# Attention steps of a pair in another order, and the last value keys turned in the middle of a projection

## The chip, the cores and the metric

The kernel runs on one core of a Trainium2 chip. The metric is the device time in microseconds (us) of one execution; the times shown are medians over several executions.

## The reference, cut to what matters

The whole computation is a hybrid block (a state-space mixer and an attention side by side, a gated feed-forward) and a second layer. The change touches the attention of the first block only: 16 heads of 64 features, 16 leading meta tokens and 1024 tokens.

```python
def block(args):
    i, qi = args
    q_pos = i * Q_BLOCK + jnp.arange(Q_BLOCK)
    valid = (key_pos[None, :] < q_pos[:, None]) & (key_pos[None, :] >= pad)
    zlog = jnp.einsum('bqhd,bkhd->bhqk', qi, kp) * scale
    log_beta = jax.nn.log_sigmoid(zlog)
    log_keep = jnp.where(valid, log_beta - zlog, 0.0)
    after = lax.cumsum(log_keep, axis=3, reverse=True) - log_keep
    w = jnp.where(valid, jnp.exp(log_beta + after), 0.0)
    return jnp.einsum('bhqk,bkhd->bqhd', w, vp)

o = lax.map(block, (jnp.arange(nb), qb))        # nb = 9 blocks of 128 queries
```

A query of block j sees the 16 meta keys and up to 128 x j others, so the nine blocks of a head are of very different length. The results of the blocks don't depend on each other. What is left of the stick after each key is a running product over the keys, and the output is a sum over keys of what is left times the step from one value to the next.

## The kernel before

TensorE is PE here, VectorE DVE, ScalarE ACT, GpSimd POOL, and SyncE (SP) issues the DMAs. Numbers are split into a high and a low half of 16 bits, so that a product of two is three matmuls (`PASSES`).

`attention_phase` works through 72 steps (`STEPS`): 8 pairs of heads (`PAIRS`), and for each the nine query blocks (`NSTEP`), j = 0 to 8 in rising order. `Step(n)` holds the numbers of a step: `p` the pair, `j` the block, `rows` (16 for j=0, else 128), `keys` = 16 + 128 j, of which at most 1024 fit in one pair of PSUM banks (`wide`); for j=8 the 16 that are left over are computed at j=3 (`z_more`) and kept in `left_more`. `slot` = j % 3 names the buffer. Each engine has a loop of its own over the steps `s`, all in program order:

- PE: `scores(s)` (queries by keys, both heads), at j=1 `turn_v` (turns the last value keys, from `steps`), then one group `linear(s + 9)` of a projection of 24 matmuls of 348 columns (`GROUPS` = 9 of them make the queries, keys and values of the next pair; in pair 7 they are those of the first w_out blocks), `turn_w(s - 1)` (turns the 32 meta columns of the step before), `values(s - 2)` (6 j matmuls on the turned left-overs, and one on the meta keys, L1274).
- ACT: `odds(s)` (sigmoid of the scores, one for each head), at j=1 `copy_v`, `left_high(s, 0)`, each third step `weight_high`, `place(s + 9)` (evicts the projection), `left_high(s, 1)` or at j=0 `values_high`, `copy_w(s - 1)`, `split_high(s - 1)`, `store(s - 2)`, at j=4 `square`.
- DVE: at j=2 `split_values`, then `split_weights(s - 2)`, `scan(s, 0)`, `scan(s, 1)` (the running product, 16 + 128 j columns), `left_low(s, 0)` or at j=0 `v_steps`, `low(s + 9)` for the queries and keys, `left_low(s, 1)` or at j=0 `values_low`, at the steps of `NORMED_AT` `norm_chunk`, each third step `weight_low`, from pair 2 at j=5 `add_square`.
- SP: `turn_left` for both heads (a transposing DMA of what is left, from one of three slots of `sent`), at j=0 `turn_values`, each third step the load of a weight block.
- POOL: the low halves of the normed chunks of the mixer's output (`low`, one for each `NORMED_AT`), and at the end the splits of two w_out blocks, each part behind a wait for a projection: `pool.wait_ge(s_lin, NT * (QKV_B + EARLY - SLOTS + s + 1))` is met when group 77 and group 80 are done, which PE does in steps 68 and 71.

What orders the engines among each other around the change:

```python
pe.wait_ge(s_keep, 2 * n)              # scores(n): odds of step n-1 are out
pe.wait_ge(s_copied, t.turn())         # turn_w(n): copy_w(n-1) has emptied turn_ps
pe.wait_ge(s_scan, 2 * n + 2)          # turn_w(n): both scans of step n
pe.wait_ge(s_copied, v_turn(p))        # turn_v(p): copy_w of the last step of pair p-1
pe.wait_ge(s_o, n)                     # values(n): store(n-1) has emptied o_ps
pe.wait_ge(*landed(t.sent(a)))         # values(n): the turned left-overs are there
pe.wait_ge(s_wlo, n + 1)               # values(n), last matmul: split_weights(n)
act.wait_ge(*landed(e - SENT_SLOTS))   # left_high: the slot of three sends ago
```

`split_weights(n)` stands on DVE at the start of step n + 2, behind all the work of step n + 1. The sends are numbered in a pair by `sent`: 17 (`SENDS`), the values first.

## Time and profile before

| | |
|---|---|
| median of 3 runs | 2336.02 us |
| lowest run | 2334.57 us |
| profiled execution | 2333.68 us, span 2331.9 us |
| PE busy | 2202.1 us, 94% |
| DVE busy | 1592.7 us, 68% |
| ACT busy | 1036.3 us, 44% |
| POOL busy | 607.0 us, 26% |
| mean granted clock of PE | 0.982 |
| attention steps, first scores to the next stage | 367.81 to 828.75 us of the span |

The page gives the busy time of an engine as a share of the span. A view of windows gives the busy time in stretches, with the clock granted to PE (1.00 is 2.4 GHz). A timeline row is a start, a length, engine, line, operation, output<-input with the shape, how many alike, and in brackets the idle time before it with what ended it. Matmuls overlap in the pipeline, so the distance from start to start tells more than a length.

### The profile page before, as it was taken

What the parts mean: (1) busy time and instruction counts of PE and PEld (TensorE: products, weight loads), DVE (VectorE), ACT (ScalarE), POOL (GpSimd) and SP (SyncE); (2) the same over time, 40 slices, a digit from 0 to 9 for tenths busy, and PEclk for the clock granted to TensorE, in tenths of its full rate; (3) what the DMA queues carried; (4) which work ended last, traced back from release to release, by engine and by line L of the source; (5) the groups of instructions that cost most, each with busy time, mean ns of one, the idle gap of its engine ahead of it and who ended that gap; (6) DMA issues with size and microseconds to landing.
All of it is one profiled execution on the core that took longest, in us unless ns stands there. A gap on an engine that the chain in (4) does not pass through costs nothing. (4 is left out here: it accounts for less than half of the span.)

```text
span 2331.9 us, 44629 instructions
## 1 busy us (share of the span) xinstructions
PE 2202.1 (94%) x18332; PEld 1411.5 (61%) x18332; DVE 1592.7 (68%) x2016; ACT 1036.3 (44%) x1883; POOL 607.0 (26%) x379
## 2 busy tenths in 40 slices
PE   7999998899999889989999999999999999999997
PEld 4666665555555556656666665458644445588846
DVE  7876887888888855787777774257688484236544
ACT  3226765667666643434444443235543232124221
POOL 3555762000000120064333331000256442001060
PEclk9999999999999989999999999999999999989998
DMA  3113213676766631211111113326333612032412
GB/s 130 48 52 101 82 55 71 116 130 125 135 126 126 110 107 63 94 41 50 55 55 59 55 51 118 101 74 212 124 102 104 212 55 82 23 101 72 158 60 73
DMA packets 279377, 216.24 MB, mean 93 GB/s; under 512 B 194752, under 2 KB 245120, under 8 KB 277776
## 3 DMA queue, kind: packets, MB, share of 16 engines
q1 hardware_dynamic: 279184, 213.51, 34.0%
q8 instruction: 140, 2.29, 0.4%
q14 instruction: 53, 0.43, 0.1%
HBM read 145.77 MB, written 25.76 MB: 74 GB/s over the span
## 5 line engine op out<-in xcount | busy, mean ns | idle before, releaser
L1519 DVE TENSOR_TENSOR_SCAN att_left<-att_left,att_unseen_prefix 16x16 f32<-16x16 f32 (+5 forms) x144 | 177.9, 1276 | 28.2 <-ACT att_left L1332 26.9
L2912 PE MATMUL ps<-second_x_hi,whi_z 128*128 128x512 f16 (+1 forms) x480 | 179.1, 373 | 2.6 <-DVE second_x_lo L1740 1.4
L1219 PE MATMUL ps<-x_hi,whi_z 128*128 128x348 f16 x560 | 176.7, 315 | 4.7 <-DVE att_q L1450 4.7
L2913 PE MATMUL ps<-second_x_lo,whi_z 128*128 128x512 f16 (+1 forms) x480 | 178.8, 372 | 0.0
L2914 PE MATMUL ps<-second_x_hi,wlo_z 128*128 128x512 f16 (+1 forms) x480 | 178.8, 372 | 0.0
L1221 PE MATMUL ps<-x_hi,wlo_z 128*128 128x348 f16 x560 | 175.3, 313 | 0.0
L1220 PE MATMUL ps<-x_lo,whi_z 128*128 128x348 f16 x560 | 175.3, 313 | 0.0
L1352 ACT ACTIVATE att_left_split<-att_left 128x256 f16<-128x256 f32 (+7 forms) x128 | 87.2, 681 | 111.9 <-DVE att_left L1519 111.1
L2215 PE MATMUL ps<-x_lo,whi_z 128*128 128x342 f16 x432 | 133.2, 308 | 0.0
L2214 PE MATMUL ps<-x_hi,whi_z 128*128 128x342 f16 x432 | 132.8, 308 | 0.0
L2216 PE MATMUL ps<-x_hi,wlo_z 128*128 128x342 f16 x432 | 132.6, 307 | 0.0
L1478 DVE SCALAR_TENSOR_TENSOR att_left_split<-att_left,att_left_split 128x256 f16<-128x256 f32 (+7 forms) x128 | 105.9, 828 | 12.7 <-ACT att_left_split L1352 12.0
L2881 POOL TENSOR_TENSOR wlo_z<-wraw_z,whi_z 128x1024 f16<-128x1024 f32 x28 | 66.3, 2367 | 178.7 <-ACT whi_z L3097 178.7
L3097 ACT ACTIVATE whi_z<-wraw_z 128x1024 f16<-128x1024 f32 x28 | 29.6, 1056 | 132.6 <-PE ps L2914 116.3
L216 PE MATMUL ps<-x_hi,whi_xbc 128*128 128x348 f16 x264 | 83.1, 315 | 4.7 <-DVE x_lo L484 4.7
L1197 POOL TENSOR_SCALAR wraw_z<-wraw_z 128x1024 f32<-128x1024 f32 x2 | 2.9, 1460 | 317.0 <-DMA wraw_z<-in_w_out 317.0
L2912 PEld LDWEIGHTS ps<-second_x_hi,whi_z 128*128 128x128 f16 x480 | 47.0, 98 | 62.4 <-issue 6.5
L217 PE MATMUL ps<-x_lo,whi_xbc 128*128 128x348 f16 x264 | 82.9, 314 | 0.0
L218 PE MATMUL ps<-x_hi,wlo_xbc 128*128 128x348 f16 x264 | 82.9, 314 | 0.0
L2913 PEld LDWEIGHTS ps<-second_x_lo,whi_z 128*128 128x128 f16 x480 | 47.1, 98 | 53.6 <-issue 3.9
L1219 PEld LDWEIGHTS ps<-x_hi,whi_z 128*128 128x128 f16 x560 | 54.8, 98 | 40.9 <-issue 13.9
L2380 DVE SCALAR_TENSOR_TENSOR wlo_z<-wraw_z,whi_z 128x512 f16<-128x512 f32 x72 | 58.2, 831 | 31.0 <-ACT whi_z L2292 31.0
(657 smaller groups left out, 6438.7 us busy)
## 6 DMA issues: line engine op xcount, KB each, us to landing
wraw_z<-in_w_second SPq DMA_DIRECT2D x30, 512.0 KB, 3.6
wraw_z<-in_w_up SPq DMA_DIRECT2D x26, 512.0 KB, 3.5
wraw_z<-in_w_qkv SPq DMA_DIRECT2D x24, 512.0 KB, 4.2
wraw_z<-in_w_down SPq DMA_DIRECT2D x20, 512.0 KB, 4.3
raw_down<-in_w_down SPq DMA_DIRECT2D x20, 512.0 KB, 4.1
seg<-dt_a_sums SPq DMA_DIRECT2D x18, 512.0 KB, 5.1
wraw_z<-in_w_up SPq DMA_DIRECT2D x36, 256.0 KB, 3.7
second_work<-parked_units SPq DMA_DIRECT2D x7, 1280.0 KB, 6.0
```

The costliest lines, as they stand in the source:

```text
L1219: nc.tensor.matmul(lin_ps(g), hi, xhi, start=(kb == 0), stop=False)
L1220: nc.tensor.matmul(lin_ps(g), hi, xlo, start=False, stop=False)
L1221: last = nc.tensor.matmul(lin_ps(g), lo, xhi, start=False, stop=(kb == DB - 1))
L1352: nc.scalar.activation(sent[:, e % SENT_SLOTS, 0:P * t.j], of_head(t, a, 0, P * t.j), ACT.Copy, scale=PSCALE).then_inc(s_left_hi, 1)
L1478: nc.vector.scalar_tensor_tensor(low_, of_head(t, a, 0, P * t.j), PSCALE, high, ALU.mult, ALU.subtract).then_inc(s_left_lo, 1)
L1519: nc.vector.tensor_tensor_scan(x, x, unseen, 1.0, ALU.mult, ALU.max).then_inc(s_scan, 1)
L2214: nc.tensor.matmul(out, hi, xhi, start=begin, stop=False, skip_group_check=True)
L2215: nc.tensor.matmul(out, hi, xlo, start=False, stop=False, skip_group_check=True)
L2216: of_block = nc.tensor.matmul(out, lo, xhi, start=False, stop=stop, skip_group_check=True)
L2912: nc.tensor.matmul(out, hi, xhi, start=(j == 0), stop=False)
L2913: nc.tensor.matmul(out, hi, xlo, start=False, stop=False)
L2914: return nc.tensor.matmul(out, lo, xhi, start=False, stop=(j == DB - 1))
```

## The change

The steps of a pair no longer run in rising order of block length. `Step` takes its block from a table by its place `i` in the pair: `ORDER` for pairs 0 to 6 and `LAST_ORDER` for pair 7. What was bound to j=0 to 5 of a pair (the value steps and their send, `turn_v`, `copy_v`, `split_values`, `square`) is bound to the same place i; `add_square` goes from place 5 to 6. The 16 left-over scores of j=8 (`z_more`) are computed at i=0 instead of at j=3 and lie at the end of the second bank. `NORMED_AT` names other steps. `turn_v` stands between the fourth and the fifth of the eight parts of the step's projection instead of ahead of it. The number, shapes and operands of all instructions stay. Of the diff, the hunks that only put `t.i` or `V_SENT[p]` in place of `t.j` or `SENDS * p` are left out.

```diff
+ORDER, LAST_ORDER = (0, 7, 2, 6, 1, 8, 3, 4, 5), (0, 7, 5, 6, 4, 8, 3, 1, 2)
+SENDS = 2 * NSTEP - 1
+
+
+def sent_order(blocks):
+
+    counts = [2 * (j > 0) + (i == 0) for i, j in enumerate(blocks)]
+    return [sum(counts[:i]) for i in range(NSTEP)]
+
+
+SENT_OF = sent_order(ORDER), sent_order(LAST_ORDER)
+V_SENT = [SENDS * p for p in range(PAIRS)]
...
-        self.n, self.p, self.j = n, n // NSTEP, n % NSTEP
+        self.n, self.p, self.i = n, n // NSTEP, n % NSTEP
+        self.j = (ORDER if self.p < PAIRS - 1 else LAST_ORDER)[self.i]
+        self.stash = self.i == 0
...
-        return SENDS * self.p + 2 * self.j - 1 + a
+        return SENDS * self.p + SENT_OF[self.p == PAIRS - 1][self.i] + a
...
-NORMED_AT = {1: 3, 2: 4, 3: 5, 10: 6, 11: 7}
+NORMED_AT = {2: 3, 4: 4, 6: 5, 11: 6, 13: 7}
...
-        z_more = flat[:, 2 * BANK:6 * BANK].rearrange("p (a n) -> p a n", a=2)[:, :, BANK:BANK + META]
+        z_more = flat[:, 2 * BANK:6 * BANK].rearrange("p (a n) -> p a n", a=2)[:, :, 2 * BANK - META:2 * BANK]
...
-                    if t.j == 3:
+                    if t.stash:
...
-                    if t.j == 1:
-                        pe.wait_ge(*landed(SENDS * t.p))
+                    if t.i == 0:
+                        pe.wait_ge(s_vlo, t.p + 1)
+                    if t.i <= 1 and t.j:
+                        pe.wait_ge(*landed(V_SENT[t.p]))
...
-                    else:
-                        pe.wait_ge(s_vlo, t.p + 1)
...
-                    if s < STEPS and ATT[s].j == 1:
+                    if s + GROUPS < (QKV_B + EARLY) * NT:
+                        linear(s + GROUPS, 0, DB // 2)
+                    if s < STEPS and ATT[s].i == 1:
                         turn_v(ATT[s].p)
                     if s + GROUPS < (QKV_B + EARLY) * NT:
-                        linear(s + GROUPS, 0, DB)
+                        linear(s + GROUPS, DB // 2, DB)
...
-                    if ATT[s].j == LAG:
+                    if ATT[s].i == LAG:
                         split_values(ATT[s].p)
...
-                    if ATT[s].j == 0:
+                    if ATT[s].j:
+                        left_low(s, 0)
+                    if ATT[s].i == 0:
                         v_steps(ATT[s].p)
-                    else:
-                        left_low(s, 0)
...
-                    if p >= 1 and ATT[s].j == 5:
+                    if p >= 1 and ATT[s].i == 6:
                         add_square(p)
```

On DVE, from the value steps of pair 3 on, to the split of the meta weights of the pair's first step (the 32x16 row; `att_left` 128x144 is block 1, 128x912 block 7). Before:

```order
L1484 TENSOR_TENSOR att_left_split<-att_v_steps,att_left_split 128x1024
L1455 SCALAR_TENSOR_TENSOR wlo_z<-wraw_z,whi_z 128x1024
L1462 TENSOR_TENSOR att_w_meta_split<-att_w_meta,att_w_meta_split 32x128
L1519 SCALAR_TENSOR_TENSOR att_left<-att_left,att_unseen_prefix 128x144 x2
L1478 SCALAR_TENSOR_TENSOR att_left_split<-att_left,att_left_split 128x128
L1450 SCALAR_TENSOR_TENSOR att_q<-ps,att_q 128x348
L1478 SCALAR_TENSOR_TENSOR att_left_split<-att_left,att_left_split 128x128
L1469 CAST att_v_meta_split<-att_v_meta 32x128
L1470 CAST att_v_meta_split<-att_v_meta 32x128
L1472 TENSOR_TENSOR att_v_meta_split<-att_v_meta,att_v_meta_split 32x128
L1462 TENSOR_TENSOR att_w_meta_split<-att_w_meta,att_w_meta_split 32x16
```

The same stretch of the changed kernel:

```order
L1500 TENSOR_TENSOR att_left_split<-att_v_steps,att_left_split 128x1024
L1471 SCALAR_TENSOR_TENSOR wlo_z<-wraw_z,whi_z 128x1024
L1478 TENSOR_TENSOR att_w_meta_split<-att_w_meta,att_w_meta_split 32x128
L1535 SCALAR_TENSOR_TENSOR att_left<-att_left,att_unseen_prefix 128x912 x2
L1494 SCALAR_TENSOR_TENSOR att_left_split<-att_left,att_left_split 128x896
L1466 SCALAR_TENSOR_TENSOR att_q<-ps,att_q 128x348
L1494 SCALAR_TENSOR_TENSOR att_left_split<-att_left,att_left_split 128x896
L1485 CAST att_v_meta_split<-att_v_meta 32x128
L1486 CAST att_v_meta_split<-att_v_meta 32x128
L1488 TENSOR_TENSOR att_v_meta_split<-att_v_meta,att_v_meta_split 32x128
L1478 TENSOR_TENSOR att_w_meta_split<-att_w_meta,att_w_meta_split 32x16
```

The block that stands between the value steps and this split has become the one of 912 columns instead of the one of 144.

On PE, where pair 3's last value keys are turned (`att_v_steps`), between the scores of the second step and its projection. Before:

```order
L1235 MATMUL ps<-att_k_odd,att_q_odd 128x144 x6
L1248 MATMUL ps<-ident,att_v_steps 32x128
L1219 MATMUL ps<-x_hi,whi_z 128x348
L1220 MATMUL ps<-x_lo,whi_z 128x348
L1221 MATMUL ps<-x_hi,wlo_z 128x348
```

In the changed kernel:

```order
L1236 MATMUL ps<-x_hi,wlo_z 128x348
L1263 MATMUL ps<-ident,att_v_steps 32x128
L1234 MATMUL ps<-x_hi,whi_z 128x348
L1235 MATMUL ps<-x_lo,whi_z 128x348
L1236 MATMUL ps<-x_hi,wlo_z 128x348
```

The turn now has twelve of the projection's matmuls ahead of it and twelve behind it.

On PE at the end of the stage, behind the last projection (the values of the last three steps). Before:

```order
L1254 MATMUL ps<-ident,att_left 32x128
L1268 MATMUL ps<-att_left_turned,att_v_tokens 64x128 x36
L1274 MATMUL ps<-att_w_meta_split,att_v_meta_split 128x128
L1254 MATMUL ps<-ident,att_left 32x128
L1268 MATMUL ps<-att_left_turned,att_v_tokens 64x128 x42
L1274 MATMUL ps<-att_w_meta_split,att_v_meta_split 128x128
L1268 MATMUL ps<-att_left_turned,att_v_tokens 64x128 x48
L1274 MATMUL ps<-att_w_meta_split,att_v_meta_split 128x128
```

In the changed kernel:

```order
L1269 MATMUL ps<-ident,att_left 32x128
L1285 MATMUL ps<-att_left_turned,att_v_tokens 64x128 x18
L1289 MATMUL ps<-att_w_meta_split,att_v_meta_split 128x128
L1269 MATMUL ps<-ident,att_left 32x128
L1285 MATMUL ps<-att_left_turned,att_v_tokens 64x128 x6
L1289 MATMUL ps<-att_w_meta_split,att_v_meta_split 128x128
L1285 MATMUL ps<-att_left_turned,att_v_tokens 64x128 x12
L1289 MATMUL ps<-att_w_meta_split,att_v_meta_split 128x128
```

Behind the last projection stand the values of blocks 3, 1 and 2 instead of those of blocks 6, 7 and 8.

## Rows read from the trace of the kernel before

**Rows 1.** The page: busy us, share of the span, instructions

```profile
PE 2202.1 (94%) x18332; PEld 1411.5 (61%) x18332; DVE 1592.7 (68%) x2016; ACT 1036.3 (44%) x1883; POOL 607.0 (26%) x379
```

**Rows 2.** Windows: pairs 0, 1, 3, then 7, tail (width, PE, PEld, DVE, ACT, POOL, clock, DMA)

```profile
367.81:423.73 55.92, 48.88 (x454) 29.64 (x449) 48.46 (x58) 35.13 (x80) 8.74 (x5) 0.94 0.47 96
423.73:482.98 59.25, 51.43 (x547) 32.20 (x542) 50.66 (x63) 38.87 (x90) 4.34 (x2) 0.97 0.68 114
...
537.06:591.14 54.08, 49.78 (x548) 31.73 (x543) 45.76 (x62) 37.05 (x88) 0.00 (x0) 1.00 0.66 127
...
753.54:809.01 55.47, 49.87 (x504) 31.07 (x498) 44.75 (x53) 33.96 (x84) 7.68 (x4) 0.97 0.61 107
809.01:828.75 19.74, 7.72 (x133) 6.21 (x131) 10.81 (x8) 7.36 (x18) 3.17 (x2) 0.65 0.61 101
```

**Rows 3.** Timeline of PE where pair 3 begins (start, length, line, idle before)

```profile
534.88 1.20 PE L1268 MATMUL ps<-att_left_turned,att_v_tokens 128*64 128x128 f16 x36 [0.26 <-ACT z L1389]
...
536.90 0.23 PE L1235 MATMUL ps<-att_k_odd,att_q_odd 64*16 64x16 f16 x6 [0.66 <-ACT att_left L1332]
...
541.72 0.28 PE L1254 MATMUL ps<-ident,att_left 128*32 128x128 f32 x1 [0.95 <-ACT att_w_meta L1345]
542.71 1.36 PE L1268 MATMUL ps<-att_left_turned,att_v_tokens 128*64 128x128 f16 x42 [0.70 <-ACT z L1389]
...
546.26 0.28 PE L1248 MATMUL ps<-ident,att_v_steps 128*32 128x128 f32 x1 [1.73 <-ACT att_w_meta L1345]
```

**Rows 4.** Timeline of PE, step 7 of pair 3, from its projection to the next scores

```profile
578.60 0.32 PE L1219 MATMUL ps<-x_hi,whi_z 128*128 128x348 f16 x1
...
582.15 0.27 PE L1254 MATMUL ps<-ident,att_left 128*32 128x128 f32 x1
582.35 1.03 PE L1268 MATMUL ps<-att_left_turned,att_v_tokens 128*64 128x128 f16 x30
...
583.47 1.47 PE L1235 MATMUL ps<-att_k_odd,att_q_odd 64*128 64x512 f16 x12
```

**Rows 5.** Timeline of DVE: block 7 of pair 2, then the value steps of pair 3

```profile
528.70 4.01 DVE L1519 TENSOR_TENSOR_SCAN att_left<-att_left,att_unseen_prefix 128x912 f32<-128x912 f32 x2
532.62 2.19 DVE L1478 SCALAR_TENSOR_TENSOR att_left_split<-att_left,att_left_split 128x896 f16<-128x896 f32 x2
...
543.31 1.19 DVE L1527 TENSOR_TENSOR att_v_steps<-att_v 128x1024 f32<-128x1024 f32 x1
...
546.08 1.22 DVE L1484 TENSOR_TENSOR att_left_split<-att_v_steps,att_left_split 128x1024 f16<-128x1024 f32 x1 [0.70 <-ACT att_left_split L1359]
547.22 1.22 DVE L1455 SCALAR_TENSOR_TENSOR wlo_z<-wraw_z,whi_z 128x1024 f16<-128x1024 f32 x1
548.47 0.28 DVE L1462 TENSOR_TENSOR att_w_meta_split<-att_w_meta,att_w_meta_split 32x128 f16<-32x128 f32 x1
```

**Rows 6.** Timeline of ACT behind the second scan of block 8

```profile
540.46 1.06 ACT L1352 ACTIVATE att_left_split<-att_left 128x1024 f16<-128x1024 f32 x1 [0.81 <-DVE att_left L1519]
541.42 0.25 ACT L1345 ACTIVATE att_w_meta<-ps 32x128 f32<-32x128 f32 x1
...
542.56 0.22 ACT L1332 ACTIVATE att_left<-ps 16x16 f32<-16x16 f32 x2
```

**Rows 7.** The line that issues turn_left, pair 7: from issue to landing

```profile
DMA to landing us min/median/max: 2.4/4.2/5.7
```

**Rows 8.** Timeline of PE, values of block 2 in pair 0

```profile
396.28 0.29 PE L1274 MATMUL ps<-att_w_meta_split,att_v_meta_split 96*128 96x128 f16 x1 [3.25 <-DVE att_w_meta_split L1462]
```

**Rows 9.** Timeline of PE, values of block 8 in the tail

```profile
824.99 2.77 PE L1268 MATMUL ps<-att_left_turned,att_v_tokens 128*64 128x128 f16 x48 [3.06 <-DMA att_left_turned<-att_left_split]
```

**Rows 10.** Timelines of DVE and POOL, block 5 of pair 7

```profile
790.30 4.26 DVE L1478 SCALAR_TENSOR_TENSOR att_left_split<-att_left,att_left_split 128x640 f16<-128x640 f32 x2
794.49 2.06 DVE L1536 TENSOR_TENSOR mixed_squares<-mixed_squares,rs_ssd_y 128x1026 f32<-128x1026 f32 x1
...
791.30 2.58 POOL L1202 TENSOR_TENSOR wlo_z<-wraw_z,whi_z 128x1024 f16<-128x1024 f32 x1
```

More of the change, by code:

```diff
@@ L1055 @@
 NORMED_EARLY = 3
-NORMED_AT = {1: 3, 2: 4, 3: 5, 10: 6, 11: 7}
+NORMED_AT = {2: 3, 4: 4, 6: 5, 11: 6, 13: 7}
 PSCALE = 32768.0
-SENDS = 2 * NSTEP - 1
 SENT_SLOTS, SENT_SIGNALS = 3, 4
@@ L1149, in turn_values @@
                 def turn_values(p):
-                    e = SENDS * p
+                    e = V_SENT[p]
                     sp.wait_ge(s_left_lo, e + 1)
@@ L1226, in scores @@
                     t = ATT[n]
-                    if t.j == 0:
+                    if t.i == 0:
                         pe.wait_ge(s_low, 2 * NT * (t.p + 1))
@@ L1259, in values @@
                         pe.wait_ge(s_o, n)
-                    if t.j == 1:
-                        pe.wait_ge(*landed(SENDS * t.p))
+                    if t.i == 0:
+                        pe.wait_ge(s_vlo, t.p + 1)
+                    if t.i <= 1 and t.j:
+                        pe.wait_ge(*landed(V_SENT[t.p]))
                     if t.j:
@@ L1325, in odds @@
                                 act.wait_ge(s_left_lo, ATT[n - 3].sent(1) + 1)
-                    if a == 1 and t.j == 3:
+                    if a == 1 and t.stash:
                         nc.scalar.activation(left_more[:, 0:META], z_more[:, 0, :], ACT.Sigmoid, scale=-0.125)
@@ L1354, in values_high @@
                 def values_high(p):
-                    e = SENDS * p
+                    e = V_SENT[p]
                     act.wait_ge(s_steps, p + 1)
@@ L1386, in store @@
                     act.wait_ge(s_pv, n + 1)
-                    if t.j == 0:
+                    if t.i == 0:
                         act.wait_ge(N.cut, t.p + 1)
@@ L1419, in _ @@
                             odds(s, a)
-                        if ATT[s].j == 1:
+                        if ATT[s].i == 1:
                             copy_v(ATT[s].p)
@@ L1429, in _ @@
                         chunk_high(NORMED_AT[s - 1])
-                    if s < STEPS:
-                        if ATT[s].j:
-                            left_high(s, 1)
-                        else:
-                            values_high(ATT[s].p)
+                    if s < STEPS and ATT[s].j:
+                        left_high(s, 1)
+                    if s < STEPS and ATT[s].i == 0:
+                        values_high(ATT[s].p)
                     if 1 <= s <= STEPS:
@@ L1439, in _ @@
                         store(s - LAG)
-                    if s < STEPS and ATT[s].p and ATT[s].j == 4:
+                    if s < STEPS and ATT[s].p and ATT[s].i == 4:
                         square(ATT[s].p - 1)
@@ L1480, in values_low @@
                 def values_low(p):
-                    e = SENDS * p
+                    e = V_SENT[p]
                     high, low_ = (sent[:, e % SENT_SLOTS, i * SEQ:(i + 1) * SEQ] for i in range(2))
@@ L1547, in _ @@
                     scan(s, 1)
-                    if ATT[s].j == 0:
+                    if ATT[s].j:
+                        left_low(s, 0)
+                    if ATT[s].i == 0:
                         v_steps(ATT[s].p)
-                    else:
-                        left_low(s, 0)
                     if s + GROUPS in SPLIT:
@@ L1555, in _ @@
                         left_low(s, 1)
-                    else:
+                    if ATT[s].i == 0:
                         values_low(ATT[s].p)
```

## Prediction

> **What bounds the kernel now.** The page's busy table comes first: TensorE (PE) is busy for 94% of the span [rows 1], so an order of steps can give back only the time in which PE waits. The windows cut by pair say how much that is in the attention stage [rows 2]: pair 0 takes 55.92 us, pair 1 59.25, each of pairs 2 to 6 takes 54.08 with 49.78 us of PE work, pair 7 takes 55.47 up to the end of its last projection, and a tail of 19.74 us with 7.72 us of PE work follows. So PE waits 4.3 us in each steady pair and 12 us in the tail, 54 us in the whole stage (widths less PE's work: 7.0 + 7.8 + 21.5 + 5.6 + 12.0).
>
> PE's timeline shows where [rows 3]: behind the longest block (j=8) at a pair's start it waits 0.26 us for ScalarE's (ACT) store, 0.95 for ACT's copy ahead of turn_w, 0.70 for the next store, and 1.73 for the copy ahead of turn_v; with 0.66 for the scores of j=0 that is 4.3. In blocks 1 to 6 there is no wait: that step is a projection of 3.55 us (578.60 to 582.15), turn_w 0.20, the values of block j, 0.165 us x j + 0.29 (j=5: 582.35 to 583.47), and the scores [rows 4].
>
> DVE's pace is behind these waits. From start to start VectorE (DVE) needs for j=7 3.92 us of scans and 2.2 of low halves, and at j=0 1.56 for v_steps, 1.14 for values_low and 1.25 for the weights' low half; each step has a split_weights of 0.3 [rows 5]. j=8 (7.0) and j=0 (5.9) are neighbours, so PE outruns DVE there. ACT sits in the loop: high half of head 1 (0.96), then copy_w, split_high and store (1.14) before it can turn the next scores into odds [rows 6].
>
> **The change, part by part.** Nothing is added or removed: the same instructions with the same shapes. PE's work stays 49.78 us a steady pair. Only waits move. I follow the three engines with the durations of rows 4 to 6 (scans and halves scaled by block length), each step counted from the end of its scores on PE, until a pair repeats itself.
>
> *Order 0,7,2,6,1,8,3,4,5.* PE step lengths without waits become 5.98 (i=0 to 1), 5.4, 4.9, 5.5, 5.8, 5.6, 5.0, 6.3, 4.9 us. In this order DVE enters i=0 3.7 us late: ACT is 3.5 us late since i=8 (j=5) ends with head 1's high half and the 1.14 us tail. From there:
> - i=0: DVE ends 5.8 us later, at 9.5 us, or 3.5 after the scores of i=1. turn_v is wanted 1.77 us (four of eight products of the projection) into i=1, and its copy_w is done at 0.8: the old 1.73 us wait is gone. It would be so even at the old place but for 0.8 us, as no j=8 stands ahead of it.
> - i=1 (j=7) and the first work of i=2: 3.92 + 2.1 + 0.45 (low) + 0.78 (split_values) + 0.17 = 7.4 us on DVE. Here the new wait arises. The values step of j=0 needs split_values and split_weights of i=0, which DVE reaches at 3.7 + 5.8 + 7.4 = 16.9 us; PE is there at 5.98 + 5.40 + 3.66 = 15.0. A wait of 1.9 us. Queued behind it on PE are the scores of j=6; for these ACT and DVE then wait, which gives DVE its time back (late by 1.7 at i=3).
> - i=3 (j=6, 3.4 + 1.7 + low and weights 2.0): DVE ends about 4.1 after the scores of i=4, PE wants the split at 4.2: no wait, or 0.35 if head 1's high half of i=2 first waits for a slot (three slots; a turn lands after a median 4.2 us [rows 7]).
> - i=4 holds ACT's square (0.94), i=5 is j=8: DVE ends at 4.8 after the scores of i=6, and the short values of j=1 want it at 4.05: 0.77 us. i=6 with weights and add_square leaves DVE at 5.5, wanted at 5.2: 0.28.
> New waits: 1.9 + 0.2 + 0.8 + 0.3 = 3.2 us a pair against 4.3 before, so 1.1 x 5 = **5.5 us** for pairs 2 to 6. A lower bound is no wait at all (21.5 us gained), an upper one is the largest that DVE's split has cost so far, 3.25 us [rows 8], in place of the 1.9 (a loss of 0.25 a pair).
>
> *NORMED_AT.* Each chunk costs DVE 1.2 us, and then POOL's low half makes a DVE instruction wait. In pair 0 they now fall on i=2, 4 and 6; the one at i=2 is followed by j=6, and by my count PE waits 1.2 + 2.3 + 2.5 + 1.2 us, with the clock at its lower level for a while as now (granted clock 0.94 in pair 0, 0.97 in pair 1, 1.00 after [rows 2]). I get 55.4 us against 55.92: **0.5**. Pair 1: waits of 1.9 + 2.8 + 1.8 and 1.0 of clock, 57.3 against 59.25: **2.0**.
>
> *LAST_ORDER 0,7,5,6,4,8,3,1,2.* In the tail of before DVE first ends j=8, its turn lands, and the 48 values products of j=8 take 2.77 us, at 1.2 GHz, the lower level, where 30 at 2.4 GHz took 1.03 (granted clock 0.65 in the tail); the wait for the turn ahead of them is 3.06 us [rows 2, 4, 9]. Now block 2 is last. After the last projection: evict and high half 0.9, DVE's low half behind POOL until about 3.8, a turn of 2.4 to 4.2, 12 products and the split 1.0 to 1.4, store and entry of the next stage 1.0: 8.2 us instead of 19.74, 11.5 less. Against it: values of 12 more block lengths run ahead of the last projection, 12 x 0.165 = 2.0; and POOL's splits of the last two w_out blocks start with fixed projections (i=5 and i=8 of pair 7). At 790 us POOL's work made DVE's two halves take 4.2 us instead of 1.55, and 0.84 more behind them: 3.5 in all [rows 10]. In before it hit j=5 and PE lost 2.2. Now it hits j=8: DVE ends at 15.0 where PE wants it at about 10: 5 us, and i=2, i=3, i=4 wait 1.05, 0.15 and 0.75. With 2 us for a clock that falls in such a wait I get 57.8 us to the end of the last projection (55.47 before) and 8.2 behind it: 66.0 against 75.2, **9.2 us**.
>
> The Trainium skill (SBUF — State Buffer, Who interferes with whom) has the port pair of these two engines as an exclusive lock, held for a whole instruction. The trace agrees: two low halves that take 1.55 us elsewhere take 4.2 beside POOL's 2.58 us subtraction. By the lock each of POOL's three instructions there could hold DVE for its whole length; at 2.58 each that would be 7.7 us instead of 3.5, and the gain would be 4.2 us smaller.
>
> Sum: 5.5 + 0.5 + 2.0 + 9.2 = 17.2 us. The profiled execution took 2333.7 us (span 2331.9); the median of the runs is 2336.0, 2.3 above it. So 2316.5 for a run like the profiled one, 2318.8 from the median; I say **2318**.
>
> **Rivals.**
> - *DVE keeps up (0.1).* ACT's lateness at i=8 is less than I count, DVE enters i=0 2 us earlier, and the waits at i=2, 6 and 7 vanish. For it: DVE's work is 45.8 us of 49.8 [rows 2]. Against it: that is 92%, and i=0 and i=1 together have 13.2 us for 11.4 of PE. Gain 21.5 + 3 + 5 + 12 = 41: 2294.
> - *Only the tail counts (0.22).* The new waits in a pair equal the old 4.3, as each late point costs 0.4 more. Then pairs 0 to 6 give nothing and pair 7 gives 5 to 10: 2328.
> - *The clock falls in each pair: slower (0.08).* Now the steady pairs keep a granted clock of 1.00 with 4.3 us of waits; pair 1 has 0.97, a price of 0.03 x 59.25 = 1.8 us [rows 2]. If the waits at i=2 and at i=6 each bring that, 14 x 1.8 = 25 us are lost against 17 gained: 2335 + 8 = 2343. It decides from 17.2 / 14 = 1.2 us a wait. Against it: 1.73 with 0.95 and 0.70 ahead of it leaves the steady clock at 1.00 [rows 2, 3], and 1.9 stands alone. The Trainium skill (TensorE: Matmul & The Clock Gate, Part 1: The HAM clock gate) says that idleness brings the throttled state, 1.2 GHz, and activity ends it; that pairs 0 and 1 and the tail lose clock and steady pairs don't agrees with it.
> - *My forecast (0.6):* 2306 to 2326.
>
> **How the numbers follow.** The forecast holds 0.6 in 2306 to 2326; with most of the tail-only case and half of the first rival the range is 2300 to 2334. A change of 2% (47 us), about what a measurement of this kernel can tell from no change, needs seven eighths of the stage's 54 us of waits: 0.03 for faster. Slower by as much needs six times the loss of the clock rival: 0.01. The rest, 0.96, is within 2%, most of it on the faster side.
>
> **What would show it.** Right: pairs 2 to 6 take 52.5 to 53.5 us; PE's longest wait in each is ahead of the values split of j=0, for DVE's split_weights, 1 to 3 us; turn_v waits for nothing; in pair 7 PE waits about 5 us in the step of j=3; 7 to 9.5 us pass from the last projection to the next stage. Wrong: if the granted clock of the steady pairs falls below 0.99; if pairs take 54 us or more; or if the wait at i=2 is absent, which would mean that ACT is not 3.5 us late at a pair's start.

## The result, and the profile after

The changed kernel takes 2318.82 us (median; 2317.35 to 2320.57), 0.993 of the kernel before, with a 95% interval of 0.9906 to 0.9954: 0.5 to 0.9% faster. Two of the four executions of the kernel before, 2565.34 and 8615.65 us, lie far off and are left out of that ratio; the other two took 2334.57 and 2336.02. The profiled execution took 2320.57 us (span 2318.8) against 2333.68 (span 2331.9), 13.1 us less. The forecast was 2318 us, yet 0.96 of its chance went to a change of less than 2%, which it took to be about what can't be told from none, and the time did change by three times what the interval allows for noise. In the long series of the experiments the kernel before had a median of 2333.7 us, so the gain is 15 to 17 us.

The windows of after, cut like those of [rows 2]: pairs 0 and 1, 2 to 6, 7, and the tail up to the first product of the next stage (width, PE, PEld, DVE, ACT, POOL, granted clock, DMA share, GB/s).

```profile
367.82:423.54 55.72, 49.53 (x490) 30.27 (x485) 50.03 (x58) 35.46 (x80) 9.39 (x4) 0.97 0.59 108
423.54:480.69 57.15, 51.57 (x548) 32.08 (x542) 51.56 (x64) 38.83 (x91) 5.05 (x2) 0.97 0.61 125
480.69:532.98 52.29, 49.79 (x548) 31.66 (x542) 45.13 (x61) 36.20 (x88) 0.00 (x0) 1.00 0.73 129
532.98:586.36 53.38, 49.85 (x548) 31.62 (x542) 46.13 (x63) 36.64 (x88) 0.00 (x0) 1.00 0.63 130
...
693.95:747.15 53.20, 49.93 (x547) 31.64 (x541) 45.99 (x62) 36.58 (x88) 0.00 (x0) 1.00 0.64 130
747.15:805.58 58.43, 52.34 (x552) 32.94 (x546) 48.60 (x57) 36.77 (x88) 9.14 (x4) 0.94 0.66 119
805.58:811.54 5.96, 2.62 (x43) 1.48 (x40) 2.73 (x3) 3.37 (x12) 3.21 (x2) 0.96 0.23 47
```

The stage lasts 443.72 us (367.82 to 811.54) against 460.94, that is 17.2 us less. Set beside [rows 2]: pair 0 gives 0.2 us, pair 1 2.1, pair 7 and the tail together 10.8 (64.39 against 75.21), and pairs 2 to 6 4.1: they take 266.5 us, 53.3 each, against 270.6. Behind the stage 4.1 us of it are lost again in this execution.

PE's waits in a steady pair (pair 3), the rows of its timeline in that window with an idle time ahead of them:

```profile
549.90 0.17 PE L1289 MATMUL ps<-att_w_meta_split,att_v_meta_split 96*128 96x16 f16 x1 [1.68 <-DVE att_w_meta_split L1478]
561.42 0.23 PE L1289 MATMUL ps<-att_w_meta_split,att_v_meta_split 96*128 96x128 f16 x1 [0.54 <-DVE att_w_meta_split L1478]
572.79 0.36 PE L1285 MATMUL ps<-att_left_turned,att_v_tokens 128*64 128x128 f16 x6 [0.33 <-ACT z L1406]
573.56 0.23 PE L1289 MATMUL ps<-att_w_meta_split,att_v_meta_split 96*128 96x128 f16 x1 [0.41 <-DVE att_w_meta_split L1478]
578.93 1.53 PE L1285 MATMUL ps<-att_left_turned,att_v_tokens 128*64 128x128 f16 x48 [0.57 <-DMA att_left_turned<-att_left_split]
```

They sum to 3.53 us and are all of the 53.38 us that isn't PE's work. The four waits and the 0.66 ahead of the scores of j=0 [rows 3] are gone, `turn_v` waits for nothing, and the largest new one stands where the prediction had it: block 0's values product (16 columns) waits 1.68 us for DVE's split.

Pair 7 from its step of j=3 on, and the tail, on PE; then what DVE and POOL did in those two places:

```profile
791.08 0.40 PE L1269 MATMUL ps<-ident,att_left 128*32 128x128 f32 x1 [2.62 <-ACT att_w_meta L1362]
795.02 0.50 PE L1234 MATMUL ps<-y_ssd_hi,whi_z 128*128 128x348 f16 x1
...
798.41 0.31 PE L1234 MATMUL ps<-y_ssd_hi,whi_z 128*128 128x348 f16 x1
...
807.72 0.36 PE L1285 MATMUL ps<-att_left_turned,att_v_tokens 128*64 128x128 f16 x6 [0.70 <-ACT z L1406]
809.39 0.23 PE L1289 MATMUL ps<-att_w_meta_split,att_v_meta_split 96*128 96x128 f16 x1 [1.32 <-DVE att_w_meta_split L1478]
810.08 0.53 PE L1285 MATMUL ps<-att_left_turned,att_v_tokens 128*64 128x128 f16 x12 [0.46 <-ACT z L1406]
811.54 0.47 PE L1867 MATMUL ps<-y_ssd_hi,whi_z 128*128 128x342 f16 x1 [0.77 <-DVEq L2006]
```

```profile
783.21 6.58 DVE L1535 TENSOR_TENSOR_SCAN att_left<-att_left,att_unseen_prefix 128x1040 f32<-128x1040 f32 x2 [1.94 <-ACT att_left L1349]
789.71 3.12 DVE L1494 SCALAR_TENSOR_TENSOR att_left_split<-att_left,att_left_split 128x1024 f16<-128x1024 f32 x2
...
807.45 2.09 DVE L1478 TENSOR_TENSOR att_w_meta_split<-att_w_meta,att_w_meta_split 32x128 f16<-32x128 f32 x2 [0.24 <-ACT att_w_meta_split L1390]
```

```profile
783.59 4.01 POOL L1217 TENSOR_TENSOR wlo_z<-wraw_z,whi_z 128x1024 f16<-128x1024 f32 x1
787.58 3.05 POOL L1212 TENSOR_SCALAR wraw_z<-wraw_z 128x1024 f32<-128x1024 f32 x1
...
807.03 2.17 POOL L1217 TENSOR_TENSOR wlo_z<-wraw_z,whi_z 128x1024 f16<-128x1024 f32 x1
```

POOL's splits now meet block 8, as forecast: its scans and low halves take 9.7 us, PE waits 2.62 us (for ACT's copy, which stands behind the high half that waits for the second scan), and comes out of the wait with products of 0.50 us where 0.31 is usual, up to about 797.3; the granted clock of 791.08 to 797.30 is 0.50. Elsewhere block 8's work on DVE looks like this (pair 3):

```profile
565.97 4.54 DVE L1535 TENSOR_TENSOR_SCAN att_left<-att_left,att_unseen_prefix 128x1040 f32<-128x1040 f32 x2 [1.94 <-ACT att_left L1349]
570.43 1.20 DVE L1494 SCALAR_TENSOR_TENSOR att_left_split<-att_left,att_left_split 128x1024 f16<-128x1024 f32 x1
...
571.98 1.21 DVE L1494 SCALAR_TENSOR_TENSOR att_left_split<-att_left,att_left_split 128x1024 f16<-128x1024 f32 x1
```

In the tail nothing waits for a turn any more; POOL's last subtraction holds DVE's two splits, 0.28 us each elsewhere, until 809.54.

### The profile page after: what moved, and what is told of

Its sections match the earlier page's. It is cut to its first block and busy times, and to the rows that moved or that the text cites. A ratio compares the mean times of both kernels' runs of the same rounds, so it can differ in the third digit from the quotient of the medians.

```text
span 2318.8 us, 44629 instructions
## 1 busy us (share of the span) xinstructions
PE 2204.9 (95%) x18332; PEld 1409.9 (61%) x18332; DVE 1588.0 (68%) x2016; ACT 1032.7 (45%) x1883; POOL 608.3 (26%) x379
## 5 line engine op out<-in xcount | busy, mean ns | idle before, releaser
L2930 PEld LDWEIGHTS ps<-second_x_hi,wlo_z 128*128 128x128 f16 x480 | 47.0, 98 | 53.4 <-issue 0.3
```

Source lines behind the costliest of these rows:

```text
L2930: return nc.tensor.matmul(out, lo, xhi, start=False, stop=(j == DB - 1))
```

## The experiments

All but e2 are edits of the changed kernel. Where a view is quoted, "pairs 2 to 6" is the stretch from the first projection of pair 2 to that of pair 7.

**e1: only LAST_ORDER.** Rising order in pairs 0 to 6, the old `NORMED_AT`, `turn_v` ahead of the projection.

```diff
-ORDER, LAST_ORDER = (0, 7, 2, 6, 1, 8, 3, 4, 5), (0, 7, 5, 6, 4, 8, 3, 1, 2)
-NORMED_AT = {2: 3, 4: 4, 6: 5, 11: 6, 13: 7}
+ORDER, LAST_ORDER = (0, 1, 2, 3, 4, 5, 6, 7, 8), (0, 7, 5, 6, 4, 8, 3, 1, 2)
+NORMED_AT = {1: 3, 2: 4, 3: 5, 10: 6, 11: 7}
```

> Rising order in pairs 0 to 6, old steps for the normed chunks, turn_v ahead of the projection; only pair 7 has the new order 0,7,5,6,4,8,3,1,2. Theory (the tail carries most of the gain): pairs 0 to 6 keep 55.9, 59.3 and 54.1 us, pair 7 and tail take 67 us against 75.2 (64.4 in the changed kernel, plus 2 to 3 us of waits behind block 8 of pair 6), ratio about 0.9965, 8 us faster. Rival (the order within pairs carries it): under 4 us faster.

2328.94 us, 0.9983 (0.9974 to 0.9993). Its windows of pair 2, pair 7 and the tail:

```profile
481.27:535.77 54.50, 49.92 (x547) 31.64 (x541) 45.75 (x62) 36.96 (x88) 0.00 (x0) 1.00 0.64 131
...
754.01:814.68 60.67, 52.96 (x587) 33.38 (x582) 50.95 (x57) 37.46 (x88) 9.43 (x4) 0.97 0.71 126
814.68:820.64 5.96, 2.62 (x43) 1.48 (x40) 2.73 (x3) 3.38 (x12) 3.21 (x2) 0.94 0.22 44
```

Pair 7 and the tail fall from 75.2 to 66.6 us, so `LAST_ORDER` alone is worth 8.6 of the 10.8. The steady pairs cost 0.4 us more than before. What differs in them are the left-over scores at i=0 and `add_square` one place later; which of the two costs it, or whether both do, wasn't separated. The stage gains 6.4 us, the kernel 4.8.

**e2: only `turn_v` amid the projection**, in the kernel before.

```diff
+                    if s + GROUPS < (QKV_B + EARLY) * NT:
+                        linear(s + GROUPS, 0, DB // 2)
                     if s < STEPS and ATT[s].j == 1:
                         turn_v(ATT[s].p)
                     if s + GROUPS < (QKV_B + EARLY) * NT:
-                        linear(s + GROUPS, 0, DB)
+                        linear(s + GROUPS, DB // 2, DB)
```

> The kernel before, with turn_v moved between the fourth and fifth part of the projection, nothing else. Theory A (the order of blocks removes the waits of a pair, turn_v's place is worth little): a steady pair stays near 54 us, as the time not waited ahead of turn_v is waited later. Theory B (turn_v's place alone removes its 1.73 us wait, and the new order trades the other waits for a new one): a steady pair takes 52.4 us, less than the 53.3 of the changed kernel; 7 x 1.7 = 12 us faster, ratio 0.995.

2329.07 us, 0.998 (0.9971 to 0.999). PE's longest waits in pairs 2 to 6, totals (line, waited for, us, times, longest):

```profile
PE ps L1268 <- DMA att_left_turned<-att_left_split: 6.6, 5, 2.2
PE ps L1268 <- ACT z L1391: 5.7, 10, 0.7
PE ps L1254 <- ACT att_w_meta L1347: 4.8, 5, 1.0
```

The wait at `turn_v` (8.7 us in five pairs before) is gone, and 6.6 us of waits for a turn that has not landed have taken its place. The steady pairs take 53.5 to 54.1 us (and one with a granted clock of 0.97, 56.1). In rising order the wait was cover for the turn of block 8. The steady pairs take 54.3 us in the mean, no less than before; most of the kernel's 4.7 us lies in pair 7, 52.34 us with a granted clock of 1.00 against 55.47 with 0.97.

**e3: the new order with `turn_v` back ahead of the projection.**

```diff
-                    if s + GROUPS < (QKV_B + EARLY) * NT:
-                        linear(s + GROUPS, 0, DB // 2)
                     if s < STEPS and ATT[s].i == 1:
                         turn_v(ATT[s].p)
                     if s + GROUPS < (QKV_B + EARLY) * NT:
-                        linear(s + GROUPS, DB // 2, DB)
+                        linear(s + GROUPS, 0, DB)
```

> The changed kernel with turn_v back ahead of the projection. Prediction's step: in the new order its copy_w comes 0.8 us after the scores of place 1, so 0.8 us of wait comes back there and the wait ahead of the values split of block 0 shrinks by as much: a steady pair stays at 53.3 us (within 0.3), the kernel within 2 us of the changed one, ratio 0.993. Rival (turn_v's place is what counts in the new order too): a pair takes 1.7 us more, 12 us slower than the changed kernel, ratio 0.998.

2319.06 us, 0.9938 (0.9921 to 0.9954), no difference from the changed kernel. Pair 3 on PE:

```profile
538.16 0.28 PE L1263 MATMUL ps<-ident,att_v_steps 128*32 128x128 f32 x1 [0.94 <-ACT att_w_meta L1360]
548.12 0.17 PE L1289 MATMUL ps<-att_w_meta_split,att_v_meta_split 96*128 96x16 f16 x1 [0.69 <-DVE att_w_meta_split L1476]
```

The 0.94 us at the turn (0.8 forecast) come off the wait for DVE's split behind it, 0.69 instead of 1.68. Over pairs 2 to 6 it is the same: PE waits 4.0 us at the turn and 7.6 for DVE's splits, 11.6 together, as in the changed kernel, which waits 11.6 for the splits alone. The profiled pairs take 53.5 us in the mean against 53.3 (pair 3 itself 54.41 against 53.38), so the place of `turn_v` is worth 0.25 us a pair at most in this order, and nothing that the times show.

**e4: the new order with the old `NORMED_AT`.**

```diff
-NORMED_AT = {2: 3, 4: 4, 6: 5, 11: 6, 13: 7}
+NORMED_AT = {1: 3, 2: 4, 3: 5, 10: 6, 11: 7}
```

> The changed kernel with the normed chunks at the old steps 1, 2, 3, 10 and 11. Theory: with chunks at steps 1 and 10, the places of block 7, the DVE backlog ahead of the values split of block 0 grows by 1.2 us and by POOL's 2.2 us in pairs 0 and 1: these two take 2 to 5 us more than 55.7 and 57.2, pairs 2 to 7 are the same. Rival (the chunks' place is worth nothing): within 0.5 us in each pair.

2322.7 us, 0.9951 (0.9934 to 0.9967), 3.9 us above the changed kernel. Windows of pairs 0 and 1:

```profile
365.92:426.35 60.43, 53.07 (x491) 31.43 (x485) 52.65 (x59) 36.64 (x82) 8.67 (x4) 0.89 0.56 101
426.35:484.81 58.46, 52.19 (x548) 32.15 (x542) 51.24 (x64) 39.24 (x92) 4.34 (x2) 0.94 0.62 120
```

The granted clock drops to 0.89 and 0.94, and the two pairs cost 6.0 us more. The new order puts block 7 where the first chunk used to be; the chunks must move with it.

**e5: LAST_ORDER and the moved turn, but rising order and the old `NORMED_AT` in pairs 0 to 6.**

```diff
-ORDER, LAST_ORDER = (0, 7, 2, 6, 1, 8, 3, 4, 5), (0, 7, 5, 6, 4, 8, 3, 1, 2)
+ORDER, LAST_ORDER = (0, 1, 2, 3, 4, 5, 6, 7, 8), (0, 7, 5, 6, 4, 8, 3, 1, 2)
...
-NORMED_AT = {2: 3, 4: 4, 6: 5, 11: 6, 13: 7}
+NORMED_AT = {1: 3, 2: 4, 3: 5, 10: 6, 11: 7}
```

> Rising order in pairs 0 to 6 with old steps for the normed chunks, but turn_v amid the projection and the new order in pair 7: the changed kernel without its order in pairs 0 to 6. Theory (behind block 8 a chain DVE, ACT, DMA stands ready, so the removed turn_v wait comes back mostly as a wait for the turn of block 8): steady pairs 53.8 to 54.3 us against 53.3 in the changed kernel, stage about 451 us against 443.7. Rival (the new order costs more than it gives): steady pairs at 52.5 us.

2327.19 us, 0.9973 (0.9961 to 0.9986): 8.4 us above the changed kernel. The steady pairs at full clock take 53.8 to 54.6 us, 54.4 in the mean, against 53.3. `ORDER` is worth about 1.1 us a steady pair, and pair 7 with its tail is 2.2 us longer, as in e1.

**e6: blocks 7 and 4 exchanged in ORDER**, so that the short block 4 stands between the value steps and block 0's split.

```diff
-ORDER, LAST_ORDER = (0, 7, 2, 6, 1, 8, 3, 4, 5), (0, 7, 5, 6, 4, 8, 3, 1, 2)
+ORDER, LAST_ORDER = (0, 4, 2, 6, 1, 8, 3, 7, 5), (0, 7, 5, 6, 4, 8, 3, 1, 2)
```

> The changed kernel with blocks 7 and 4 swapped in pairs 0 to 6: order 0,4,2,6,1,8,3,7,5. Theory (the wait ahead of the values split of block 0 is DVE's backlog of value steps and block 7): with block 4 there DVE has 2.5 us less to do, the wait of 1.7 us vanishes; block 7 at place 7 makes DVE late for the values split of block 3, about 1 us of wait: steady pairs at 52.4 to 52.9 us instead of 53.3, 3 to 5 us faster than the changed kernel. Rival (that wait has another cause, a fixed chain behind the value steps): it stays at 1.5 us or more and the pair takes 54 us or more.

2321.5 us, 0.9946 (0.9929 to 0.9963), 2.7 us above the changed kernel. The 1.7 us wait is gone, as the prediction's account of it requires, but the pairs take 54.3 us in the mean. Waits of ACT, then of PE, in pairs 2 to 6:

```profile
ACT att_left_split L1369 <- DMA att_left_turned<-att_left_split: 10.0, 9, 1.7
...
PE ps L1285 <- ACT z L1406: 6.9, 11, 0.7
PE ps L1289 <- DVE att_w_meta_split L1478: 4.0, 10, 0.7
```

So the wait has the cause that was given, and taking it away doesn't shorten the pair. PE waits 17.5 us in the five pairs against 16.8 in the changed kernel (widths less its work), and ACT waits 10.0 us for slots of `sent` to land. Most of the 1.0 us by which the pairs are longer is not a wait: PE's own work is 0.9 us a pair longer, and two of the pairs have a granted clock of 0.97.

**e7: without POOL's low halves of the last two w_out blocks** (they are left out).

```diff
-                    nc.gpsimd.tensor_scalar(hi, raw, 1.0, 1.0, ALU.mult, ALU.mult).then_inc(Lo.step, 1)
-                    pool.wait_ge(Lo.step, 2 * s + 2)
-                    nc.gpsimd.tensor_tensor(lo, raw, hi, ALU.subtract).then_inc(Lo.cut, 1)
+                    nc.gpsimd.tensor_scalar(hi, raw, 1.0, 1.0, ALU.mult, ALU.mult).then_inc(Lo.cut, 1)
```

> The changed kernel with one part left out: POOL's subtraction that makes the low halves of the last two w_out blocks (two instructions, 2.1 us each when alone); what they would write stays as it was. Theory (POOL holds DVE out during block 8 of pair 7): the two scans of block 8 take 4.6 instead of 6.6 us, PE's wait there shrinks from 3.2 to about 1 us and the clock does not fall, pair 7 takes 54 to 56 us instead of 58.4, 3 us less in all. Rival (the wait there comes from block 8 alone): pair 7 stays within 1 us of 58.4.

2317.52 us, 0.9929 (0.9909 to 0.9949), 1.3 us under the changed kernel, where 3 were expected and the changed kernel's runs lie 3.2 us apart. Pair 7's window, and the wait of the step of j=3:

```profile
748.11:804.88 56.77, 49.99 (x552) 31.71 (x546) 46.98 (x57) 36.82 (x88) 5.38 (x3) 1.00 0.68 123
```

```profile
791.13 0.28 PE L1267 MATMUL ps<-ident,att_left 128*32 128x128 f32 x1 [1.52 <-ACT att_w_meta L1360]
```

The wait falls from 2.62 to 1.52 us and the granted clock rises from 0.94 to 1.00, so POOL's subtraction causes 1.1 us of the wait, and without it the clock holds. The two scans shrink by the same 1.1 us, to 5.48; in the steady pairs they take 4.54. So of the 1.52 us that are left about 0.9 can be put down to POOL's cast and scaling, which stayed, and 0.6 to the place of block 8 itself (an estimate from these scans; no run left all of POOL's work out). PE works 2.35 us less in the pair, which is the price of that clock; as PE comes sooner to later waits (1.19 us at the next turn), only 1.7 us of the pair's length is gained. The tail gains nothing, 6.05 us against 5.96: DVE's two splits aren't held any more, and PE waits for the turn of block 2 instead:

```profile
809.09 0.85 PE L1283 MATMUL ps<-att_left_turned,att_v_tokens 128*64 128x128 f16 x12 [1.54 <-DMA att_left_turned<-att_left_split]
```

**e8: 0.55 us more on DVE ahead of block 0's split.**

```diff
                     nc.vector.tensor_copy(again, vm[:, :])
+                    for i in range(6):
+                        nc.vector.tensor_copy(more[:, i, :], vm[:, i * META:(i + 1) * META])
```

> The changed kernel with six more small copies (32x16, about 0.17 us each, to a tile that nothing reads) on DVE at place 2 of each pair, ahead of the split that PE waits for. Theory (that wait is DVE's backlog): the wait of 1.7 us grows by the 1.0 us, each steady pair takes 0.8 to 1.0 us more, 6 to 8 us in all. Rival (DVE has slack there): under 0.3 us a pair.

2318.64 us, 0.9934 (0.9913 to 0.9954), but these are two runs of 2314.55 and 2322.73 us (mean clock 0.988 and 0.980), so the time settles nothing here; the trace is of the first. The six copies take 0.55 us of DVE and PE's wait grows by just that:

```profile
549.93 0.17 PE L1290 MATMUL ps<-att_w_meta_split,att_v_meta_split 96*128 96x16 f16 x1 [2.23 <-DVE att_w_meta_split L1479]
```

Yet pairs 2 to 6 take 53.2 us, one of them with a granted clock of 0.97. The step of block 1 (place 4) no longer waits, and ACT's waits for slots fell:

```profile
ACT att_left_split L1370 <- DMA att_left_turned<-att_left_split: 1.6, 1, 1.6
```

In the changed kernel that row reads as follows (here of pairs 2 to 6; the trace of before has no such wait in its pairs 2 to 6):

```profile
ACT att_left_split L1369 <- DMA att_left_turned<-att_left_split: 6.2, 7, 1.6
```

6.2 us in five pairs is 1.24 us a pair: `left_high` waits for the landing of three sends ago. That gave a new theory, L, of what sets a pair's length.

**e9: four slots for the sends.** Their room comes from value steps computed in place; what else it changes or leaves out stands in the expectation.

```diff
-SENT_SLOTS, SENT_SIGNALS = 3, 4
+SENT_SLOTS, SENT_SIGNALS = 4, 5
-        steps, first_v = sb("v_steps", [P, T + META]), sb("v_first", [P, 2, NSTEP])
+        steps, first_v = v, sb("v_first", [P, 2, NSTEP])
```

> The changed kernel with four slots for the sent left-overs in place of three. The room comes from value steps that are computed in place over the values; the kernel leaves out the right difference and the right first value there (it subtracts a value from itself, and takes the first value from a constant), with the same instructions and shapes. Theory L (a pair's length is set by the loop through the slots: ScalarE's high half of block 2 waits for a turn of three sends ago, which is why an added wait at block 0's split did not lengthen the pair): no high half of pairs 2 to 6 waits for a landing (four such waits of 0.34 to 1.41 us in the changed kernel), the wait at block 0's split stays at 1.7 us, and the mean of pairs 2 to 6 falls from 53.3 to 52.6-52.9 us. Rival D (VectorE's pace sets the pair, the slot wait is slack): the landing waits go, the pairs stay at 53.3, and the waits of TensorE reappear ahead of VectorE's splits.

2310.65 us, 0.9904 (0.9876 to 0.9933). No high half waits for a landing, and the pairs take 52.0 us, 1.27 less than in the changed kernel: about the 1.24 us that ACT waited there, and more than the 0.4 to 0.7 expected, which came from the four waits that the timeline's rows had shown; the grouped waits have seven. The wait at block 0's split, expected to stay at 1.7 us, is 1.68 in pair 5 and 0.5 to 0.9 in the four others. PE's waits in pairs 2 to 6:

```profile
PE ps L1289 <- DVE att_w_meta_split L1478: 5.8, 9, 1.7
PE ps L1285 <- DMA att_left_turned<-att_left_split: 5.4, 7, 1.4
```

**e10: 0.55 us less on DVE at the same place**, with three slots (the second copy and the low part of the meta values are left out from pair 2 on).

```diff
+                    if p >= 2:
+                        nc.vector.tensor_copy(high, vm[:, :]).then_inc(s_vlo, 1)
+                        return
                     nc.vector.tensor_copy(high, vm[:, :]).then_inc(s_vhi, 1)
```

> The changed kernel without two of the three instructions of split_values from pair 2 on (0.55 us on VectorE ahead of block 0's split, the mirror image of the run that added as much); it leaves out the low part of the meta values. Both theories: the wait at block 0's split falls from 1.68 to about 1.1 us. Theory L: ScalarE's slot waits at block 2 grow by as much and pairs 2 to 6 stay at 53.3 us. Rival D: each pair is 0.5 us shorter, 52.8.

2319.38 us, 0.9937 (0.9914 to 0.9959). In pair 3 PE's wait falls to 0.78 us, and the pair takes 53.34. The mean of the pairs is 53.4 us, but it holds two pairs with a granted clock of 0.97 (54.1 and 55.5) and two of 52.7 and 51.6, so that this run does not settle it: PE's work in the five pairs is 252.9 us against 249.6, and its waits are 14.3 against 16.8. By the waits alone the pairs gave back 0.51 us each, nearly all of the 0.55, and PE's slower work took it again. ACT's waits for slots grew to 8.6 us:

```profile
ACT att_left_split L1369 <- DMA att_left_turned<-att_left_split: 8.6, 6, 2.7
```

**e11: e9 and e10 together.**

> Four slots and 0.55 us less on VectorE ahead of block 0's split, with what both kernels leave out. Theory L: with the slot wait gone, VectorE's work counts there, and the pairs are 0.5 us shorter than with four slots alone, 52.1-52.4 us. Rival D: 52.8, the same as with the work taken away alone. If a third thing sets the pair, all three kernels have 53.3 us, and TensorE's waits only move.

2307.56 us, 0.9891 (0.9863 to 0.992). The pairs take 51.4 us, 0.58 less than with four slots alone, for 0.55 us of DVE's work; with three slots the same 0.55, added (e8) or taken away (e10), moved the mean by -0.06 and +0.14 us. With four slots the reading is clean: PE's work is the same in both (248.9 and 248.8 us in the five pairs), and the 0.58 us are all wait. With three slots it is not, as e8 and e10 have pairs with a lower clock. e8 shows that DVE's work could grow there without a longer pair; that taking it away gains nothing because the slots bind fits theory L and the times (2319.38 us in e10, 2318.82 in the changed kernel), but isn't shown apart from the clock. Both came out 0.6 to 1.0 us a pair below the figures expected of theory L, for the reason given at e9.

**e12: four slots with the whole computation.** The first values are copied first, the last steps go to a buffer of 32 columns, and the long difference is written over the values.

```diff
-        steps, first_v = sb("v_steps", [P, T + META]), sb("v_first", [P, 2, NSTEP])
+        steps, last_steps, first_v = v, sb("v_last_steps", [P, 2 * META]), sb("v_first", [P, 2, NSTEP])
...
+                    nc.vector.tensor_copy(first_v[:, p % 2, :], v[:, 0:SEQ + 1:P]).then_inc(s_first, 1)
+                    nc.vector.tensor_tensor(last_steps[half(0), 0:META], v[half(0), SEQ + 1:T + 1], v[half(0), SEQ:T], ALU.subtract)
...
+                    dve.wait_ge(s_first, p + 1)
+                    nc.vector.tensor_tensor(steps[:, 0:SEQ], v[:, 1:SEQ + 1], v[:, 0:SEQ], ALU.subtract).then_inc(s_steps, 1)
```

> The whole computation with four slots for the sent left-overs: the value steps are computed in place over the values (first the copy of the first values, then the last steps into a buffer of their own of 32 columns, then the long difference), which frees the 4.2 KB that the fourth slot takes. Theory L (the loop through the slots sets a pair's length): as with four slots and a wrong difference, pairs 2 to 6 take 52.0 us in the mean against 53.3, no high half of them waits for a landing, and the time is about 2310.5 us, 8 us under the changed kernel. Rival: the wait of the long difference for the copy of the first values, and the place of that copy ahead of it, put 0.1 to 0.3 us on VectorE in each pair, which counts one to one now that the slots don't bind: 52.3 us a pair, 2312 us.

2310.74 us (2309.12 to 2313.39), 0.9902 (0.9885 to 0.9918) of the kernel before, 8.1 us under the changed kernel. Windows of pairs 3 and 4, then all of PE's waits in pairs 2 to 6:

```profile
531.36:583.45 52.09, 49.77 (x547) 31.62 (x541) 45.70 (x62) 36.43 (x88) 0.00 (x0) 1.00 0.65 132
583.45:635.61 52.16, 49.83 (x547) 31.63 (x541) 45.77 (x62) 36.43 (x88) 0.00 (x0) 1.00 0.66 133
```

```profile
PE ps L1289 <- DVE att_w_meta_split L1478: 8.1, 9, 1.7
PE ps L1285 <- DMA att_left_turned<-att_left_split: 3.0, 5, 1.4
```

The wait at block 0's split is still 1.68 us in pair 3. In the changed kernel PE's waits of those five pairs were 11.6 us for DVE's split, 2.6 for a turn, 2.1 for a store and 0.4 for a copy; now they are 8.1 and 3.0, 5.6 us less, and ACT's 6.2 us of slot waits are gone. This is the fastest version that computes everything, and the long difference's own wait costs nothing that shows.

## Why the prediction was right, and where it was wrong

**The step that failed** stands in "How the numbers follow": "A change of 2% (47 us), about what a measurement of this kernel can tell from no change". That bound came from no row and no time of the case. The measurement has an interval of 0.24% to either side, 5.6 us, and the runs of the changed kernel lie within 0.14% of each other. The prediction's own sum, 17.2 us, is three times that, and even its rival "only the tail counts" (2328) is outside it (e1 and e2, 4.8 us under the kernel before, were still told from it). By its own cases a gain that can be measured had to get about 0.9 and no change 0.1 or less, in place of 0.96 for the latter.

**The sum** was met in the stage, 17.2 us against 17.2, but by terms whose errors cancel: 4.1 + 0.2 + 2.1 + 10.8 measured, 5.5 + 0.5 + 2.0 + 9.2 forecast. That the two agree to a tenth is luck.
- *Pairs 2 to 6*: 4.1 us, not 5.5. PE waited for 3.5 us in pair 3, not 3.2. The wait at block 0's split was 1.68 us (1.9 forecast), its cause as told (e6, e8). At place 4 it was 0.54 (0 to 0.35), at place 6 0.33 + 0.41 (0.77), at place 7 0.57 (0.28), the last for a turn's landing and not for DVE.
- *What sets a pair's length* was not seen. The prediction had the three slots only as "0.35 if head 1's high half of i=2 first waits for a slot", at one place, and counted the 1.9 us wait at its full price. The runs show that with three slots that wait has no price of its own: without it PE waits no less in the pair (e6), and 0.55 us more of it doesn't lengthen the pair (e8). A fourth slot is worth 1.3 us a pair (e9, e12). The trace of before couldn't show it, as no high half of its steady pairs waits for a slot; but [rows 7] has a turn landing after up to 5.7 us, and the new order sends block 7's two halves and block 2's first within about 4 us of each other.
- *`turn_v`*: the old place would have cost 0.8 us; e3 shows 0.94, and that it comes off the next wait.
- *`NORMED_AT`*: pair 0 gave 0.2 (0.5 forecast), pair 1 2.1 (2.0). Left where it was it would have cost 6.0 us in these pairs (e4); the prediction didn't price that.
- *Pair 7*: 58.43 us, 57.8 forecast. The terms named there don't add up to 57.8: 49.87 of PE's work, 2.0 of values, 5 + 1.95 of waits and 2 for the clock are 60.8, or 59.2 with the work as it is at full clock (48.23, pair 7 of e2). Measured were 50.0 of work at full clock (e7), 6.1 of waits and 2.35 for the clock. So the terms were near; that 57.8 came nearer than their sum is luck. "5 us" of wait in the step of j=3 were 2.62 + 0.58. The scans and low halves of block 8 lost 2.75 us to POOL (6.58 + 3.12 against 4.54 + 1.20 + 1.21 in the steady pairs), where 3.5 was taken. The clock's price was 2.35 us by e7, 2 forecast. The Trainium skill (SBUF — State Buffer, Who interferes with whom) has the port pair as an exclusive lock; that it is held for the whole instruction is said there of DVE's two-port modes. DVE's loss of 2.75 us beside 8.1 us of POOL's work doesn't bear out the 7.7 us that the prediction drew from it; POOL's own subtraction took 4.01 us there and 2.17 in the tail, so POOL waited as well.
- *The tail*: 5.96 us, 8.2 forecast. The low half was to sit behind POOL until 3.8 us; it was through 1.6 us after the last projection, just as POOL's subtraction began, and no one waited for its turn. Only the two small splits were held, by 1.5 us, and that cost nothing: without it (e7) PE waits 1.54 us for the turn and the tail lasts 6.05. The 8.2 took the lower end of each of its own ranges; their upper ends give 10.4.
- *Behind the stage*: a term that the sum lacked. The next stage used to begin at full clock, behind 48 values products. It now begins behind short ones and small waits, and at half clock at first:

```profile
811.54:823.40 11.86, 11.86 (x72) 7.58 (x73) 2.46 (x2) 3.30 (x3) 0.00 (x0) 0.88 0.64 221
```

```profile
828.75:839.20 10.45, 10.45 (x72) 7.04 (x73) 2.45 (x2) 3.31 (x3) 0.00 (x0) 1.00 0.71 251
```

The first row is of after, the second of before, each from the stage's first product over 72 products: 1.4 us more, with a granted clock of 0.88 instead of 1.00. Over the first 10.45 us the granted clock is 0.86 here and 0.79 to 0.87 in all eleven experiments that have the short tail; e2, which keeps the old one, has 1.00. The other 2.7 us that this execution lost behind the stage were not traced to one place. Around 1000 us, where the two programs are the same but out of step with each other, its granted clock fell lower than that of before (0.89 against 0.94 from 1000 to 1030 us), and other runs of the changed kernel with a mean clock of 0.987 instead of 0.983 are 3 us shorter; that this is one effect is only argued.

**The rivals.** "Only the tail counts" fell with e5. "DVE keeps up" fell: DVE's split is still waited for. "The clock falls in each pair" fell as told, all five steady pairs of the profiled execution keep 1.00; a weaker form of it lives, since e2, e5, e6, e8 and e10 each have one or two steady pairs with 0.97, at 1.2 to 2.3 us where the pair is longer for it at all (those of e6 and e8 are not). So a sum of waits that a pair bears in one run can cost clock in another.

## What to carry to other kernels

Before saying that a gain can't be measured, put it against the scatter of the times at hand, not against a round figure. When work is put in another order, list for every ring of buffers how close together its users now come, and set that against the landing times, also where the old order never waited for the ring; a wait in a chain of in-order engines has a price only if no other wait takes it up, and adding and removing the same small work, with and without the suspected limit, tells which it is, if PE's own work is the same in the runs compared. A short tail is worth most of its length, but look at the clock that the next stage starts with.

## What the hardware showed

The turns of left-overs took from 2.3 to 6.7 us from issue to landing (median 3.7) for blocks 1 to 8, and one ring slot more for them was worth 8.1 us of a kernel whose PE is busy for 95% of the span. POOL and DVE slowed each other: a subtraction of 128x1024 on POOL took 4.01 us beside two scans that took 6.58 instead of 4.54, and two 32x128 splits of 0.28 us each took 2.09. And a single wait of 2.62 us, with 0.58 behind it, was followed by some 6 us at half rate (791.1 to 797.3), while the waits of 1.68 us in the steady pairs were not in this execution.
